# One layer of a hybrid attention encoder on one core: softmax and delta-rule attention interleaved, short convolution and head norms moved into the input products

## The chip, the core and the metric

The kernel runs on one core of a Trainium2 chip. The metric is the device time of one execution in microseconds (us). The engines are called PE (TensorE matmul; PEld is its weight load), DVE (VectorE), ACT (ScalarE), POOL (GpSimd) and SP (the queue that issues most loads). Each engine runs its own instructions in order and waits for others by semaphores. Operands live in SBUF; PE writes PSUM, which has eight banks here, LP 0 to 3 and MP 0 to 3.

## The reference, cut to what matters

Two layers are computed for 512 prompt frames and 32 sample frames (N = 544 tokens), width 1024, all float32. Only the first layer's mixer is touched. Cut to its core:

```python
qkv_a, z_a, b_a, a_a, q_b, k_b, v_b, f_b = split(rmsnorm(x) @ w_in)
qkv_a = silu(causal_conv(qkv_a, width 4))           # 12 rows of 128 channels
qa, ka = l2norm(qa), l2norm(ka)                     # 4 heads each: 8 rows
oa = gated_delta_rule(qa, ka, va, g, beta, s0)      # chunks of 64 tokens, WY form
oa = rmsnorm(oa) * silu(z_a)
ob = fox_attention(q_b, k_b, v_b, log_forget)       # softmax, 4 heads, blocks of 128 queries
x = x + concat(oa, ob) @ w_out
```

Per chunk and head the delta rule inverts a 64x64 triangular matrix (here by doubling: blocks of 2, 4, ... 32), forms u and w with it, and then carries a 128x128 state from chunk to chunk. Everything behind this mixer (cross-attention, MLP, the second layer) is the same before and after.

## The kernel before

**Weights.** A product with a 1024-row weight is made in panels of 256 columns (two tiles of 128 columns). SP loads a panel into `stage`, ACT copies its high part to `wh` (`split`, L1291), POOL subtracts to get the low part `wl` (`low_parts`, L616), and PE makes each tile with three products per 128 rows (`block`, L717). There are two slots of each, so the split of a panel is made right after the product of the panel two before it. A tile may begin once the tile two before it has been drained from LP by DVE (L768).

**Stages of the first mixer, in order.** (1) `in_a`: 16 tiles; DVE drains 12 rows into `ua` (`four_conv_rows`, L1936) and 4 into `z`; 48 small gate products stand after the fourth tile (L895). (2) `in_b`: 12 tiles into kb_f, vb_f, qb_f; behind each drain DVE makes the 4-tap convolution of one `ua` row into `sq` (L1998 to L2016, eight instructions), and ACT applies Silu (L1470), which needs an activation table of its own (loads at L1450 and L1479). Between the panels PE transposes k and v (`turned`, L909). (3) `forget_rows(False)` (L936) sums the log-forget rows on PE, and the cached keys are transposed (L971). (4) `attention("fox_p")`: 16 units of softmax attention, and beside them, through the hooks `delta_sums`, `delta_rstds` and `delta_scales` (L978, L1501, L2018), the l2norm of the 8 q and k rows. (5) `forget_rows(True)`, (6) `attention("fox_s")`: 4 units for the sample tokens. (7) The delta rule: chunk sums (L1002), then the list `DELTA` (L446), which every engine walks in the same order: 63 steps `inv` of the inverses (`inverse`: gram, turns, x and d per size, uw), 19 steps `turn` (`turn_in`: transposes and forget rows, through one bank), 36 steps `rec` (`recurrence`: ws, qs, ds, o per chunk). The last 16 steps are the recurrence of tiles 2 and 3 alone. (8) `out0`: the first half of the products can run at once; the other half waits for the norm and gate of the delta output (L1624 on ACT, L1113 on DVE).

**Softmax pipeline.** `attention` (L794 on PE, L1337 on ACT, L1815 on DVE) runs over i: PE transposes the probabilities of unit i-2, multiplies values of i-3, makes scores of i+1; DVE scales the scores (L1843), masks, takes the maximum, later normalises; ACT takes the exponential (L1347) and copies (L1370, L1379). Scores, transposes and values each alternate between two banks.

Of the kernel before, what the change touches and what calls it, by code (L numbers as in the profile page):

```python
# [5 lines left out]
def build_program(nc, t):  # L6
# [71 lines left out]
    with ctx:  # L78
# [20 lines left out]
        xl = place("xl", [128, KT, N], f32r)  # L99
        stage = [place(f"stage{s}", [128, 2048]) for s in range(2)]  # L100
# [85 lines left out]
        def region(at):  # L186
# [19 lines left out]
        delta_buf, delta_end = region(delta_at)  # L206

        LT, Tm, TmT, Xm = [[delta_buf(f"{n}{c}", [128, H, 64 if c < 2 else NS]) for c in range(3)]
                           for n in ("LT", "Tm", "TmT", "Xm")]
        BT = [delta_buf(f"BT{c}", [128, 2, H, 64 if c < 2 else NS]) for c in range(3)]  # L210
        dec = Xm
        AT = [delta_buf(f"AT{j}", [128, H, 64 if j < TT else NS]) for j in range(NTOK)]

        kd = [place(f"kd{j}", [128, H, 128], at=xh_at + 4 * H * 128 * j) for j in range(TT)] + [
            delta_buf("kd_s", [128, H, 128])]
        vbt = [place(f"vbt{j}", [128, H, 128], at=xl_at + 4 * H * 128 * j) for j in range(TT)] + [
            delta_buf("vbt_s", [128, H, 128])]
        um = [place(f"um{j}", [128, H, 128], at=xl_at + 4 * H * 128 * j) for j in range(TT)] + [
            delta_buf("um_s", [128, H, 128])]
        assert 4 * H * 128 * TT <= 4 * H * N  # L220
        at = delta_end[0]
        kbe = [delta_buf(f"kbe{j}", [128, H, 128]) for j in range(NTOK)]
        wT = [place(f"wT{j}", [128, H, 128 if j < TT else NS], at=at + 4 * H * 128 * j) for j in range(NTOK)]
        grow = delta_buf("grow", [128, 2, H, 128])
        vnew = delta_buf("vnew", [128, H, 128])

        S = delta_buf("S", [128, 4, H, 128])
        gsm = delta_buf("gsm", [128, NTOK, 16])
        neg_g = delta_buf("neg_g", [128, NTOK, H])
        eg = delta_buf("eg", [128, NTOK, 2, H])  # L230
        o_a = ua[:, 2 * H:3 * H, 0:N]
        assert delta_end[0] <= gates_start, (delta_end[0], gates_start)
# [74 lines left out]
        neg_ready = sem("neg_ready")  # L307
# [99 lines left out]

        def out_bank(U, u):
            bank = MP[0:U["D"], 2 + u % 2, 0:U["P"] * U["G"]]
            return bank.rearrange("p (g n) -> p g n", g=U["G"]) if U["G"] > 1 else bank  # L410
# [14 lines left out]
        def steps_of(j):  # L425
            sizes = sizes_of(j)
            pe = ["gram", "turns"]
            dve = ["lower", "gram"]
            for n in sizes:
                pe += [f"x{n}"] + ([f"dt{n}"] if n != sizes[-1] else []) + [f"dtt{n}"]  # L430
                dve += ([f"dt{n}"] if n != sizes[-1] else []) + [f"dtt{n}"]
            return pe + ["uw"], ["gram", "turns"] + [f"x{n}" for n in sizes] + ["uw"], dve
# [3 lines left out]
        def count_of(steps, name, r):  # L436
# [4 lines left out]
        TURNS = [(kind, j) for kind in ("k", "v", "g") for j in (0, 1, TT)] + [  # L441
            ("w", 0), ("w", 1)] + [(kind, j) for kind in ("g", "k", "v", "w") for j in (2, 3)]
# [3 lines left out]
        def delta_order():  # L446
# [3 lines left out]
            turns = [("turn",) + t for t in TURNS if t[0] != "w"]  # L450
            recs = [("rec", name, j, c) for j, c in CHUNKS for name in ("ws", "qs", "ds", "o")]
            for r, tiles in enumerate(((0, 1, TT), (2, 3))):
                names = ["gram", "turns"] + [f"{w}{n}" for n in SIZES for w in ("x", "d")] + ["uw"]
                later = [x for x in recs if r and x[2] in (0, 1, TT)]
                for i, name in enumerate(names):
                    for j in tiles:
# [4 lines left out]
                        if name == "uw" and j < TT:  # L461
                            out.append(("turn", "w", j))
# [11 lines left out]
        def inv_bank(j, k):  # L474

            return LP[:, 2 * STREAM[j] + k, :] if j < TT else MP[:, 2 + k, :]
# [31 lines left out]
        def _(sp):  # L508
# [70 lines left out]
            first_pair("out0")  # L579
# [5 lines left out]

            sp.wait_ge(arena_free, 1)
# [20 lines left out]
        def _(pool):  # L607
# [79 lines left out]
            with pool.Fori(2, LIN["out0"][0] // 2 + 1) as i:  # L687
# [20 lines left out]
            with pool.Fori(LIN["out0"][0] // 2 + 1, PANELS // 2) as i:  # L708
# [5 lines left out]
        def _(pe):  # L714
# [79 lines left out]
            def attention(name, also=lambda i: None):  # L794
                u0, count = GROUP[name]

                def scores(u):
                    U = UNITS[u]
                    if u >= 2:
# [1476 lines left out]
```

## Time and profile before

| | us |
|---|---|
| median of 3 runs (1750.8 to 1761.66) | 1759.62 |
| the profiled execution, its own time | 1760.79 |
| its span in the trace | 1759.0 |
| PE busy, PEld busy | 1667.0, 1568.5 |
| DVE, ACT, POOL busy | 765.3, 607.2, 531.3 |

The span runs from the first to the last instruction of the trace; the execution's own time is 1.8 us more. A busy share of PE counts a matmul from its start to its modelled end. Times inside the trace are given from the span's start. The stretches of the first mixer in it: in_a 36.3 to 127.7, in_b to 211.9, forget rows and cached keys to 232.8, fox_p to 275.9, forget rows to 291.8, fox_s to 310.4, delta rule to 436.4 (its first round of inverses to 362.6, the second with recurrence steps between to 418.8, the last recurrence steps alone to 436.4), then out0.

### The profile page before, as it was taken

To read this page: it belongs to the slowest core of one execution; us is meant where nothing else is said; L and a number is where in the kernel's file an instruction comes from. 1 tells how busy PE (TensorE), PEld (TensorE's weight loads), DVE (VectorE), ACT (ScalarE), POOL (GpSimd) and SP (SyncE) were. 2 spreads that over 40 slices of the span, in tenths; PEclk is the share of its full clock that TensorE was granted. 3 is DMA by queue.
4 is the path that set the end of the run, shared out by engine and by line. 5 is a ranking of instruction groups with operands and counts; after the bars stand their busy time and mean duration, and the time that the engine had idled before them with its cause. 6 is when DMAs were issued, how large, how long until landed. Compare 5 with 4: busy or idle time off the path is not lost.

```text
span 1759.0 us, 31567 instructions
## 1 busy us (share of the span) xinstructions
PE 1667.0 (95%) x13326; PEld 1568.5 (89%) x13326; DVE 765.3 (44%) x1403; ACT 607.2 (35%) x1120; POOL 531.3 (30%) x187
## 2 busy tenths in 40 slices
PE   6999888999988999999999999989889999999998
PEld 6999756888887899999999997559878999999998
DVE  4119753443574632222223623784746322223235
ACT  4113373221443442222223314783434323222232
POOL 4533300210252133443433432002621443433441
PEclk9999998899999999999999998899999999999999
DMA  5232300000433023223222223001320223222221
GB/s 150 74 95 76 119 26 1 8 2 13 144 114 103 25 72 97 82 87 96 89 78 95 73 96 133 1 1 49 120 97 25 80 89 97 90 78 95 81 86 51
DMA packets 123034, 131.39 MB, mean 75 GB/s; under 512 B 6285, under 2 KB 115122, under 8 KB 122930
## 3 DMA queue, kind: packets, MB, share of 16 engines
q1 hardware_dynamic: 116064, 123.27, 21.5%
q10 hardware_dynamic: 6866, 6.63, 1.2%
q8 instruction: 77, 1.26, 0.3%
q14 instruction: 27, 0.22, 0.0%
HBM read 122.44 MB, written 7.45 MB: 74 GB/s over the span
## 4 chain that ended last, share of the span: by engine, by line
PE 84%; DVE 10%; ACT 3%; issue 2%; DMA 0%; ACTq 0%; DVEq 0%
PE LP L722 66%; PE MP L839 3%; PE LP L1044 3%; PE LP L805 3%; PE MP L823 2%; DVE acc L1790 1%; DVE sq L2014 1%; PE LP L957 1%; DVE sq L2012 1%; DVE xl L1797 1%; PE MP L1138 1%; DVE probs L1856 1%; PE MP L1124 1%; PE MP L1132 0%; DMA stage<-in_w_in_ab 0%
## 5 line engine op out<-in xcount | busy, mean ns | idle before, releaser
L619 POOL TENSOR_TENSOR wl<-stage,wh 128x2048 fp32r<-128x2048 f32 x107 | 493.5, 4612 | 1017.5 <-ACT wh L1294 1017.4
L722 PE MATMUL LP<-xh,wh 128*128 128x272 f32 x2176 | 458.3, 292 | 14.3 <-DVE xl L1797 7.2
L722 PE MATMUL LP<-xh,wl 128*128 128x272 f32 x2176 | 452.9, 290 | 0.0
L722 PE MATMUL LP<-xl,wh 128*128 128x272 f32 x2176 | 452.3, 290 | 0.0
L1294 ACT CAST wh<-stage 128x2048 fp32r<-128x2048 f32 x107 | 203.7, 1904 | 462.7 <-PE LP L722 461.9
L722 PEld LDWEIGHTS LP<-xh,wh 128*128 128x128 f32 x2176 | 345.6, 190 | 19.3 <-DVE xl L1797 9.7
L722 PEld LDWEIGHTS LP<-xl,wh 128*128 128x128 f32 x2176 | 345.7, 191 | 0.0
L722 PEld LDWEIGHTS LP<-xh,wl 128*128 128x128 f32 x2176 | 342.9, 190 | 0.0
L722 PE MATMUL LP<-hh,wh 128*128 128x272 f32 x1024 | 211.2, 287 | 0.0
L722 PE MATMUL LP<-hh,wl 128*128 128x272 f32 x1024 | 210.6, 288 | 0.0
L722 PE MATMUL LP<-hl,wh 128*128 128x272 f32 x1024 | 210.3, 287 | 0.0
L2176 DVE TENSOR_TENSOR hsq<-rel 128x544 f32<-128x544 f32 x64 | 70.1, 1095 | 267.9 <-ACT rel L1701 261.4
L722 PEld LDWEIGHTS LP<-hl,wh 128*128 128x128 f32 x1024 | 160.1, 188 | 0.0
L722 PEld LDWEIGHTS LP<-hh,wh 128*128 128x128 f32 x1024 | 159.4, 188 | 0.0
L722 PEld LDWEIGHTS LP<-hh,wl 128*128 128x128 f32 x1024 | 159.4, 188 | 0.0
L2191 DVE TENSOR_TENSOR dtmp<-LP,rstd 128x544 f32<-128x544 f32 x64 | 46.3, 724 | 234.8 <-PE LP L722 234.8
L1701 ACT ACTIVATE rel<-LP 128x544 f32<-128x544 f32 x64 | 39.9, 624 | 237.3 <-PE LP L722 237.3
L1790 DVE TENSOR_TENSOR acc<-acc,sq 128x544 f32<-128x544 f32 x49 | 81.8, 1670 | 23.4 <-ACT sq L1319 23.4
L1797 DVE SCALAR_TENSOR_TENSOR xl<-x,cols,xh 128x544 fp32r<-128x544 f32 x48 | 78.4, 1644 | 23.9 <-ACT xh L1324 23.7
L1319 ACT ACTIVATE sq<-x 128x544 f32<-128x544 f32 x56 | 36.8, 658 | 138.2 <-DVE x L1811 75.0
L699 POOL TENSOR_TENSOR BT<-LT,level 128x256 f32<-128x256 f32 (+1 forms) x24 | 18.1, 768 | 160.8 <-DVE LT L2076 132.3
L823 PEld LDWEIGHTS MP<-ident,probs 128*128 128x128 f32 (+2 forms) x284 | 32.2, 151 | 30.8 <-DVE probs L1887 19.5
(357 smaller groups left out, 1877.7 us busy)
## 6 DMA issues: line engine op xcount, KB each, us to landing
stage<-in_w_up SPq DMA_DIRECT2D x32, 1024.0 KB, 5.3
stage<-in_w_down SPq DMA_DIRECT2D x32, 1024.0 KB, 5.2
stage<-in_w_in_ab SPq DMA_DIRECT2D x13, 1024.0 KB, 5.2
stage<-in_w_xkv SPq DMA_DIRECT2D x8, 1024.0 KB, 5.4
stage<-in_w_in_c SPq DMA_DIRECT2D x6, 1024.0 KB, 5.0
stage<-in_w_out_ab SPq DMA_DIRECT2D x4, 1024.0 KB, 7.1
stage<-in_w_xq SPq DMA_DIRECT2D x4, 1024.0 KB, 5.6
stage<-in_w_xo SPq DMA_DIRECT2D x4, 1024.0 KB, 5.9
```

What stands on the lines that cost most here:

```text
L619: pool.tensor_tensor(wl[s][:, :], stage[s][:, :], wh[s][:, :].bitcast(f32), ALU.subtract).then_inc(w_lo, 1)
L722: mm = pe.matmul(LP[:, 2 * slot + half, 0:b - a], weights, X[part][:, k, a:b], start=(first and n_ == 0), stop=(last and n_ == 2), skip_gr ...
L805: mm = pe.matmul(LP[0:U["P"], 2 * (u % 2) + at // 512, at % 512:at % 512 + n], U["q"][g], kT, start=True, stop=True, skip_group_check=True)
L823: mm = pe.transpose(MP[0:n, u % 2, to:to + P], probs_of(u, slice(at, at + n)), ident[0:P, 0:P])
L839: mm = pe.matmul(MP[0:U["D"], 2 + u % 2, g * P:g * P + w], v[g], U["PT"][0:n, u % 2, at:at + w], start=(c == 0), stop=(c == last), skip_gr ...
L1044: return pe.matmul(out, lhsT, rhs, start=start, stop=stop, skip_group_check=True)
L1294: act.copy(wh[s][:, :], stage[s][:, :]).then_inc(w_hi, 1)
L1701: act.activation(rel[:, k % 2, :].rearrange("p (a n) -> p a n", a=2), LP[:, 2 * (k % 2):2 * (k % 2) + 2, 0:HALF], ACT.Relu).then_inc(relu_ ...
L1790: dve.tensor_tensor(acc[:, :], acc[:, :], sq[:, k % 2, :], ALU.add).then_inc(sq_used, 1)
L1797: dve.scalar_tensor_tensor(out=xl[:, k, :], in0=x[:, k, :], scalar=gain(n_, k), in1=xh[:, k, :].bitcast(f32), op0=ALU.mult, op1=ALU.subtra ...
L2176: dve.tensor_tensor(hsq[:, k % 2, :], rel[:, k % 2, :], rel[:, k % 2, :], ALU.mult).then_inc(hsq_ready, 1)
L2191: dve.tensor_tensor(two(dtmp[:, k % 2, :]), banks(k), two(rstd[:, :]), ALU.mult).then_inc(drained, 1)
```

## The change

**Layout and banks.** The buffers of the delta rule move into `stage`, `wh` and `wl`, so that softmax and delta rule can be live together; kbe, wT, vbt and um lie in `ua` itself. So the first two panels of `out0` are loaded only after the last turn. The inverse has one bank per tile (MP 0, 1), turns have MP 3, the recurrence MP 2 and LP 3; softmax has LP 0 for scores, LP 1 for transposes, LP 2 for values, one each. The two updates of a doubling step become one DVE instruction; q and w become turns of their own (25 turns).

**Input products.** The convolution and Silu of each row go behind its drain in `in_a`; the l2norm goes into `in_b`, its PE sums in the panel breaks.

**Attention.** One walk: `attention` gets a hook `beside`, which runs 6 steps of DELTA in each of 18 rounds of fox_p, and the last 16 steps in 6 rounds of fox_s.

```diff
+        LATE = [x for x in DELTA if x[0] == "rec" and x[2] in (2, 3)]
+        BESIDE = {"fox_p": spread(DELTA[:len(DELTA) - len(LATE)], 0, 18), "fox_s": spread(LATE, 0, 6)}
+        def beside(name, inverse, turn_in, recurrence):
+            def go(i):
+                for what in BESIDE[name].get(i, ()):
+                    {"inv": inverse, "turn": turn_in, "rec": recurrence}[what[0]](*what[1:])
+            return go
...
-            first_pair("out0")
...
+            sp.wait_ge(turn_used, len(TURNS))
+            first_pair("out0")
...
                 def scores(u):
-                    if u >= 2:
+                    if fox:
+                        pe.wait_ge(sc_used, u)
+                    elif u >= 2:
...
                     pe.wait_ge(p_ready, u + 1)
-                    if u >= 2:
+                    if fox:
+                        pe.wait_ge(pt_ready, u)
+                    elif u >= 2:
...
-            one_pair("in_b", 0, XS)
-            pe.wait_ge(conv_dve, 1)
+            pe.wait_ge(conv_dve, CW * NCONV)
...
+            def head_sums(first, last):
+                def go():
+                    for f in range(first, last):
+                        pe.wait_ge(head_sq, f + 1)
+                        if f >= 2:
+                            pe.wait_ge(head_ln, f - 1)
+                        for half, (a, b) in enumerate(TOKENS):
+                            mm = pe.matmul(MP[:, 2 * (f % 2) + half, 0:HALF], ones[:, :], sq[:, f % 2, a:b], ...)
+                        mm.then_inc(head_sum, 1)
+                return go
+            one_pair("in_b", 0, XS, between=head_sums(0, 2))
+            head_sums(2, 5)()
+            one_pair("in_b", 1, XS, between=head_sums(5, 2 * H))
+            pe.wait_ge(head_ln, 2 * H)
...
-            attention("fox_p", delta_sums)
-            pe.wait_ge(head_ln, 2 * H)
-            forget_rows(True)
-            attention("fox_s")
...
+            attention("fox_p", beside("fox_p", inverse, turn_in, recurrence))
+            forget_rows(True)
+            pe.wait_ge(rows_act, 2 * H)
+            attention("fox_s", beside("fox_s", inverse, turn_in, recurrence))
...
-            product("in_a")
+            act.preload_act_table_set("silu_and_others")
+            for T in range(NCONV + H):
+                if T % 2:
+                    split_after("in_a", T)
+                if 1 <= T <= NCONV:
+                    act.wait_ge(conv_dve, CW * T)
+                    act.activation(ua[:, T - 1, 0:N], sq[:, (T - 1) % 2, :], ACT.Silu).then_inc(conv_act, 1)
+            act.wait_ge(drained, DRAINED["in_b"])
+            act.activation(z[:, :, :], z[:, :, :], ACT.Silu).then_inc(conv_act, 1)
+            act.preload_act_table_set("natural_log_exp_and_others")
...
+            split(0, 16 * (LIN["out0"][0] // 2 + 1))
+            attention("fox_s", beside("fox_s", inverse, turn_in, recurrence))
...
                     head_rstd(2 * H + h - 1, 1.0 / HD)
+                if h == 1:
+                    split(1, 16 * (LIN["out0"][0] // 2 + 1))
...
+                dve.tensor_copy(conv_new[:, 0, :, f], ua[:, f, NPT:NPT + PAD])
+                dve.tensor_copy(conv_new[:, 1, :, f], ua[:, f, UPAD - PAD:UPAD])
+                for i in range(CW):
...
                 dve.tensor_tensor(two((kb_f, vb_f, qb_f)[f // H][:, f % H, :]), banks(f), two(rstd[:, :]), ALU.mult)
-                for i in range(CW):
...
+                for m in {2: (0, 1), 4: (2, 3, 4), 6: (5, 6, 7)}.get(f, ()):
+                    dve.wait_ge(head_exp, m + 1)
+                    dve.scalar_tensor_tensor(out=ua[:, m, 0:N], in0=ua[:, m, 0:N], in1=head_squares[:, m % 2, :], ...)
```

`spread(items, first, steps)` cuts a list into `steps` nearly equal parts. On ACT a row's norm in `in_b` is `row_rstd` (Ln and Exp into `head_squares`) and `head_square`; rows 0 and 1 are squared before `in_b`'s loop, the norms of rows 0 and 1 stand after tile 1, of 2 to 4 after tile 3, of 5 to 7 after tile 5. On DVE, fox_p begins after the chunk sums have come back from ACT.

## Rows read from the trace of the kernel before

**Rows 1.** The page: busy shares, and the chain that ended last
```profile
PE 1667.0 (95%) x13326; PEld 1568.5 (89%) x13326; DVE 765.3 (44%) x1403; ACT 607.2 (35%) x1120; POOL 531.3 (30%) x187
...
PE 84%; DVE 10%; ACT 3%; issue 2%; DMA 0%; ACTq 0%; DVEq 0%
```
**Rows 2.** Stretch, its length, busy PE PEld DVE ACT POOL, clock; stages in order
```profile
36.30:127.70 91.40, 91.29 (x728) 89.38 (x728) 13.12 (x41) 13.37 (x7) 45.54 (x53) 1.00 0.30 93
127.70:211.90 84.20, 80.21 (x622) 79.26 (x622) 73.53 (x120) 27.62 (x37) 28.23 (x6) 0.96 0.24 77
211.90:232.80 20.90, 13.54 (x48) 8.63 (x49) 8.30 (x9) 8.05 (x11) 4.50 (x1) 0.84 0.27 101
232.80:275.90 43.10, 34.66 (x184) 25.59 (x184) 32.60 (x104) 33.37 (x96) 0.00 (x0) 0.96 0.07 27
275.90:291.80 15.90, 15.72 (x72) 11.32 (x72) 0.00 (x0) 2.06 (x6) 0.00 (x0) 0.89 0.00 1
291.80:310.40 18.60, 15.50 (x76) 11.80 (x76) 8.84 (x28) 5.68 (x22) 0.00 (x0) 0.72 0.00 1
310.40:362.60 52.20, 49.03 (x860) 42.95 (x860) 22.36 (x54) 13.59 (x45) 9.37 (x14) 0.86 0.03 8
362.60:418.80 56.20, 55.91 (x849) 49.51 (x848) 25.21 (x59) 12.25 (x33) 8.72 (x10) 0.95 0.01 2
418.80:436.40 17.60, 15.76 (x130) 14.88 (x128) 7.23 (x20) 1.99 (x5) 0.00 (x0) 1.00 0.00 1
436.40:453.10 16.70, 13.73 (x63) 11.59 (x64) 8.64 (x12) 9.82 (x16) 0.00 (x0) 0.80 0.84 283
397.00:412.00 15.00, 15.00 (x256) 13.70 (x256) 6.74 (x18) 2.07 (x5) 0.23 (x1) 1.00 0.01 2
```
**Rows 3.** Timeline of DVE in in_a: drain of a row (first and last), two drains of z
```profile
36.30 0.43 DVE L1941 TENSOR_TENSOR ua<-LP,rstd 128x272 f32<-128x272 f32 x1
37.22 0.44 DVE L1941 TENSOR_TENSOR ua<-LP,rstd 128x272 f32<-128x272 f32 x1
...
109.70 0.72 DVE L1954 TENSOR_TENSOR z<-LP,rstd 128x544 f32<-128x544 f32 x1 [5.03 <-PE LP L722]
115.71 0.72 DVE L1954 TENSOR_TENSOR z<-LP,rstd 128x544 f32<-128x544 f32 x1 [5.29 <-PE LP L722]
```
**Rows 4.** Timeline of DVE in in_b: a convolution's first instruction, the next drain, a long instruction
```profile
137.69 0.48 DVE L2008 TENSOR_SCALAR sq<-ua,cols 128x512 f32<-128x512 f32 x1
...
141.09 0.72 DVE L2000 TENSOR_TENSOR kb_f<-LP,rstd 128x544 f32<-128x544 f32 x1
...
144.01 4.59 DVE L2014 SCALAR_TENSOR_TENSOR sq<-ua,cols,sq 128x32 f32<-128x32 f32 x1
```
**Rows 5.** Timeline of POOL: low parts of a panel in in_a and in in_b
```profile
105.67 4.61 POOL L619 TENSOR_TENSOR wl<-stage,wh 128x2048 fp32r<-128x2048 f32 x1 [7.34 <-ACT wh L1294]
...
143.74 4.81 POOL L619 TENSOR_TENSOR wl<-stage,wh 128x2048 fp32r<-128x2048 f32 x1 [9.41 <-ACT wh L1294]
```
**Rows 6.** Timeline of PE: k turns, forget rows, the sums of one head row
```profile
181.43 1.03 PE L915 MATMUL MP<-ident,kb_f 128*32 128x128 f32 x4 [3.21 <-ACT k_out L1459]
...
222.96 7.21 PE L957 MATMUL LP<-upper,gates_raw 128*128 128x512 f32 x16 [5.71 <-ACT nF L1484]
...
250.72 1.16 PE L987 MATMUL LP<-head_squares,ones 128*128 128x272 f32 x4 [0.45 <-ACT rstd L1512]
```
**Rows 7.** Timeline of DVE in out0: the first head's norm and gain
```profile
443.66 0.78 DVE L2117 SCALAR_TENSOR_TENSOR ua<-ua,cols,rstd 128x544 f32<-128x544 f32 x1 [7.56 <-ACT rstd L1540]
```
**Rows 8.** Groups in fox_p: busy, mean ns, idle before and its releaser
```profile
L1843 DVE SCALAR_TENSOR_TENSOR probs<-LP,nF 128x128 f32<-128x128 f32 (+3 forms) x16 | 7.8, 485 | 13.8 <-PE LP L805 13.8
L1851 DVE TENSOR_REDUCE nm<-probs 128x1 f32<-128x128 f32 (+3 forms) x16 | 7.7, 480 | 0.0
L1848 DVE TENSOR_TENSOR probs<-probs,diag_mask 128x128 f32<-128x128 f32 x16 | 4.6, 285 | 0.0
...
L1347 ACT ACTIVATE probs<-probs,nm 128x128 f32<-128x128 f32 (+3 forms) x16 | 9.0, 562 | 6.4 <-DVE nm L1851 6.3
...
L1379 ACT CAST xh<-MP 128x128 fp32r<-128x128 f32 x16 | 4.0, 250 | 0.4 <-PE MP L839 0.4
...
L1347 ACT ACTIVATION_READ_ACCUMULATOR probs<-probs,nm 128x1 f32 x16 | 3.0, 188 | 0.0
```
**Rows 9.** Groups over 0 to 560: the delta rule's copy of x
```profile
L1601 ACT COPY Xm<-LP 128x256 f32<-128x256 f32 x20 | 7.2, 373 | 27.9 <-PE LP L1044 27.6
```

More of the change, by code:

```diff
@@ new lines, in build_program, with in_rows @@
+        um_s = place("um_s", [128, H, 128], at=stage_at + 5 * slot + 4 * H * 128)
+        wT_s = place("wT_s", [128, H, NS], at=stage_at + 5 * slot + 8 * H * 128)
+        vnew = sample_buf("vnew", [128, H, 128])
+        assert sample_end[0] <= stage_at + 6 * slot
+        def in_rows(first):
+            return [ua[:, first:first + H, 128 * j:128 * j + 128] for j in range(TT)]
+        kbe, wT, vbt, um = (in_rows(H) + [kbe_s], in_rows(H) + [wT_s], in_rows(2 * H) + [vbt_s], in_rows(2 * H) + [um_s])
@@ L449, in delta_order @@
             out = []
-            turns = [("turn",) + t for t in TURNS if t[0] != "w"]
+            turns = [("turn",) + t for t in TURNS if t[0] not in "qw"]
             recs = [("rec", name, j, c) for j, c in CHUNKS for name in ("ws", "qs", "ds", "o")]
@@ L472, in build_program, with inv_bank, spread @@
         assert sum(x[0] == "turn" for x in DELTA) == len(TURNS)
-        def inv_bank(j, k):
-            return LP[:, 2 * STREAM[j] + k, :] if j < TT else MP[:, 2 + k, :]
+        def inv_bank(j):
+            return MP[:, STREAM[j], :]
+        TURN_BANK, W_BANK, O_BANK = MP[:, 3, :], MP[:, 2, :], LP[:, 3, :]
+        def spread(items, first, steps):
+            return {first + i: items[len(items) * i // steps:len(items) * (i + 1) // steps] for i in range(steps)}
+        LATE = [x for x in DELTA if x[0] == "rec" and x[2] in (2, 3)]
[5 more added lines that the diff above has]
+            return go
         def chunks_of(j):
@@ L685, in _ @@
             assert n[0] == MASKS, n[0]
-            with pool.Fori(2, LIN["out0"][0] // 2 + 1) as i:
+            with pool.Fori(2, LIN["out0"][0] // 2) as i:
                 for s in range(2):
@@ L706, in _ @@
                     level_mask(what[2], SIZES.index(int(what[1][1:])) + 1)
[L708 removed]
+            with pool.Fori(LIN["out0"][0] // 2, PANELS // 2) as i:
                 for s in range(2):
@@ L1369, in pt @@
                     full = sum(n_ == 128 for n_, _ in U["v"])
-                    inst = act.copy(U["PT"][:, s, 0:full * w], MP[:, s, 0:full * w])
+                    bank = LP[:, 1, :] if U["kind"] == "fox" else MP[:, s, :]
+                    inst = act.copy(U["PT"][:, s, 0:full * w], bank[:, 0:full * w])
                     if full < len(U["v"]):
                         rows = U["v"][-1][0]
-                        inst = act.copy(U["PT"][0:rows, s, full * w:full * w + w], MP[0:rows, s, full * w:full * w + w])
+                        inst = act.copy(U["PT"][0:rows, s, full * w:full * w + w], bank[0:rows, full * w:full * w + w])
                     inst.then_inc(pt_ready, 1)
@@ L1611, in recurrence @@
                     act.wait_ge(rec_pe, 4 * CHUNKS.index((j, c)) + 4)
[L1612 removed]
+                    act.copy(o_a[:, :, a:a + P], O_BANK[:, 0:H * P].rearrange("p (h n) -> p h n", h=H)
                              ).then_inc(rec_act, 1)
[L1615 to L1616 removed]
+            attention("fox_p", beside("fox_p", inverse, turn_in, recurrence))
+            act.wait_ge(ol_ready, sum(GROUP["fox_p"]))
+            forget_rows(True)
+            split(0, 16 * (LIN["out0"][0] // 2 + 1))
+            attention("fox_s", beside("fox_s", inverse, turn_in, recurrence))
+            act.wait_ge(ol_ready, sum(GROUP["fox_s"]))
             act.wait_ge(rec_dve, 2 * len(CHUNKS))
             store(t["o_p_gdn_state"][0, 0].rearrange("h k v -> k h v"), S[:, 0, :, :])
[L1619 removed]
+            store(t["o_s_gdn_state"][0, 0].rearrange("h k v -> k h v"), S[:, 1, :, :])
             act.wait_ge(rec_act, NTOK)
```

456 lines of the change are left out of this document (212 added, 244 removed).

## The prediction

> **What bounds the kernel now.** The page first: PE is busy for 95% of the span, and 84% of the chain that ended last is PE [rows 1]. So time can come only from stretches where PE waits, runs at the lower clock, or does work that goes. The busy time by stretch gives them [rows 2]. In in_a PE is full (91.29 of 91.40 us), a tile comes each 6.01 us (z drains at 109.70 and 115.71) and DVE is idle for 78 us [rows 3]. In in_b DVE is busy for 73.53 of 84.20 us, since the convolution is there. Between in_b and fox_p PE works 13.54 of 20.90 us. From fox_p to the end of the delta rule (232.8 to 436.4, 203.6 us) PE is busy for 186.5 us and its weight loads for 156.0: little idle time, at a mean clock below 1. The change touches nothing behind out0, so the sum is that of six stretches.
>
> **1. in_a: the convolution comes in, +6 us.** Per row DVE now drains (36.30 to 37.22, 0.92 us [rows 3]), copies two edges (my estimate 0.25, from two small instructions; 0 to 0.5) and convolves (137.69 to 141.09, 3.40 us [rows 4]): 4.57 us, 9.1 per panel of two tiles, below the 12.0 that PE needs. But an instruction of POOL takes DVE's time. The low part of a panel runs 4.6 us, and a 128x32 convolution step that met one took 4.59 us where its neighbours take a quarter of one; a z drain from PSUM at 109.70 inside POOL's 105.67 to 110.28 took its usual 0.72 [rows 3 to 5]. So DVE loses up to 4.4 us a panel and needs 13.5. PE runs 12.0. The lag is bounded: tile 13 may start at 109.7 once row 11 is drained. DVE starts at 36.3; eleven rows (50.3), one drain (0.9), the gate row (0.7), six low parts in the way (4.2 each, 25) and some 3.5 for POOL's small mask instructions give 116.7, so PE loses 7.0; with 0.92 of a drain hidden under each low part it is 1.5. I take 6, nearer the full block; range +1 to +9. Silu on ACT (12 times 0.66) has room there: ACT is busy for 13 of 91 us.
>
> **2. in_b: the convolution goes, the head norms come, +6 us.** DVE falls to a drain a tile. PE gains 8 rows of sums. One takes 1.16 us with its tail, some 1.0 in a stream [rows 6]: +8.0. They stand between panels, and PE waits in two places for a square that ACT makes only after the split (1.9), Ln, Exp and Square (0.65 each) with 2 or 3 sums in between: 1.9 each, +3.8 (0 to 6). What goes: PE's 3.21 us wait for ACT at the k turns [rows 6], since ACT no longer sits behind a Silu, and the lower clock that followed it (tile 8 was made in 182.4 to 190.7, 8.3 for 6.0): -5.5. Together +6.3, range +1 to +10. The gate chain at in_b's start stays: POOL's low part holds it today as well, and ACT's Silu of z fits beside.
>
> **3. Forget rows, first time, -4 us.** PE waited 5.71 us there for ACT, which was behind the last convolution [rows 6], and ACT loaded a table. Now: eight long matmuls a head, 2.3 us, 9.2 for four; 0.8 before; key turns through two banks with ACT copies 3.0; the chunk sums 2.7, their way through ACT and DVE 1.4: DVE's first softmax step at 17.1 after the last drain instead of 21.4. -4.3, and the sums' 2.9 leave the delta rule. Range -2 to -7.
>
> **4. fox_p beside the delta rule, -11.5 us.** Before: 43.1 + 52.2 + 56.2 = 151.5 us [rows 2]. PE's work in it, from the timeline at the full clock: softmax per head 2.2 scores, 1.4 transposes, 2.5 values, 24.4 for four heads (the head sums are gone); first round of inverses 42 (52.2 less the chunk sums, 4.5 of waiting and 8 from the lower clock); second 53. With some 4 us for the switches: 124, 6.9 a round over 18 rounds. What is added are waits. Softmax has one bank each, so scores of i+1 wait for DVE's scaling of i, which stands behind DVE's delta work of the round before: about 0.6 to 0.8 us a round after PE's transposes and values (1.0) are done. An ACT copy of a delta step stands behind the exponential, which waits for scaling, mask and maximum (0.49 + 0.29 + 0.48 [rows 8]); PE's three or four items before it mostly cover that. In the first round DVE has three tiles' chains of five instructions before its next scaling: 3 us. 18 x 0.75 + 3 = 16.5: 140 us. Queued behind such a wait on PE is all of the round's delta work, so nothing fills it. DVE has 27 + 48 of 140 us, ACT less; neither binds. Range 128 to 160 us, so -23 to +8.
>
> The page Perfetto Trace Analysis of the Trainium skill (Identifying the Most-Contended Engine) says to judge TensorE by the busy share of its weight loads, because pipelined matmuls hide gaps. By that, 203.6 - 156.0 = 48 us would be idle in the whole block, not 17. The trace agrees only in part: in 397 to 412, where PE never waits, the loads are busy for 13.70 of 15.00 us [rows 2], so 156.0 stand for 171. That row carries the first rival below.
>
> **5. Forget rows and fox_s with the last recurrence, 0 us.** Before 15.9 + 18.6 + 17.6 = 52.1. PE's work in the last two is 28 at the full clock, but the chain is short of cover: four units over six rounds. The first out0 panel is now split here and its low part runs in DVE's way. That no row shows for these operations; the nearest are the blocked step and the free drain [rows 4, 3]: +0 to +4.4. I take the block, since mask and normalisation have both inputs in SBUF or are of the kind that met it: 36 for 36. Range -8 to +5. The page SBUF — State Buffer of the Trainium skill (Who interferes with whom) says that a VectorE instruction with two SBUF inputs waits for the whole of a GpSimd instruction that reads SBUF, a reduction does not; by that the mask is held and the maximum waits behind it in the queue too, the same 4.4.
>
> **6. Start of out0, +4.4 us.** The second split (1.9) now stands between the norms of the heads, and its low part (4.6) follows right after DVE's first gain at 443.66 [rows 7]. The second comes at 450 instead of 445.5. Covered today: both panels were split long before. Range +1 to +6.
>
> **Sum:** 6 + 6.3 - 4.3 - 11.5 + 0 + 4.4 = +0.9. The profiled execution took 1760.8 (1759.0 and 1.8 around it), 1.2 above the median 1759.6; 1761.7 by its clock, 1760 as a median. So no change that a measurement of this kernel can tell (about 1%, 17.6 us).
>
> **Rivals.** *A: PE runs solid.* Delta steps cover softmax's waits and the clock stays up: 124 in part 4, 28 in part 5: 16 and 8 less; half of parts 1 and 2 with it, 6: 1730. For it: 171 of 203.6 us, and DVE's small load. Against: one bank each, and a strict order on four engines.
> *B: the round boundary decides.* PE gets its first delta step only when the whole chain has run: a DVE delta step (0.7), scaling, mask, maximum (0.49, 0.29, 0.48), exponential (0.56 and 0.19 for its sum), softmax's copy (0.25) and the delta copy (0.37) [rows 8, 9]: 3.3 us, less the 1.0 of softmax work on PE beside it, is 2.3, 1.6 more than the 0.75 in my sum. Over 24 rounds +38: 1798. It decides from 0.75 us more a round (+17.6). For it: in fox_s such a chain leaves PE at a clock of 0.72 [rows 2]. Against: six items stand between, and most need no copy of their own round.
> *C: DVE binds the input products.* Every low part blocks fully and PE falls behind by 1.5 a panel in in_a, with part 6 at its upper end: +10 more than my sum in all, 1771, still within 1%.
> *D: the interleaving gives nothing*, PE being 95% busy already: part 4 is 151.5 less the chain sums' 2.9, 148.6, and part 5 as now: 1769.
>
> **Chances.** Forecast 0.32, C 0.1, D 0.1 (these three within 1%, less their tails), A 0.26, B 0.22. Range 1733 to 1787; the forecast's own 1748 to 1773. Faster 0.27, same 0.49, slower 0.24.
>
> **What would show it.** In the changed profile in_a ends 3 to 9 us later with DVE as PE's releaser once or twice; convolution steps of 4.6 us stand in in_a; in_b has two waits of PE for `sq`; the fused fox_p lasts 135 to 147 us with the clock above 0.95 and waits of PE for `probs` or `nm` below 1 us each; DVE's second gain in out0 comes 6 us after the first. Wrong if the fused part is below 128 (A) or above 160 (B), or if PE's idle time in in_a is nil.

## The result, and the profile after

The changed kernel takes 1813.42 us (median of 4, 1810.11 to 1816.63), the kernel before 1760.64 (median of 4): a ratio of 1.031 with an interval of 1.025 to 1.036, 53 us slower. The forecast was 1760, the range 1733 to 1787; it lies outside. The profiled execution took 1816.63 us, its span is 1814.8 against 1759.0.

The page first, to hold beside [rows 1]: the engines' busy times and the chain that ended last.

```profile
PE 1695.8 (93%) x13326; PEld 1591.6 (88%) x13326; DVE 763.7 (42%) x1406; ACT 611.1 (34%) x1112; POOL 533.7 (29%) x187
...
PE 85%; DVE 10%; issue 2%; ACT 2%; DMA 0%; ACTq 0%; DVEq 0%
```

The number of matmuls is the same (13326), and PE is busy for 28.8 us more, at a mean granted clock of 0.949 for 0.966. So the page already tells that idle time alone cannot explain the 56 us, and points to the clock. The stretches of the changed kernel, as in [rows 2] (length, busy time of PE, PEld, DVE, ACT and POOL, granted clock, DMA share, GB/s): in_a, in_b, forget rows and cached keys, fox_p with 108 delta items, forget rows, fox_s with the last recurrence, start of out0.

```profile
36.00:132.60 96.60, 92.35 (x733) 90.01 (x732) 77.16 (x161) 21.54 (x20) 49.02 (x54) 1.00 0.29 88
132.60:224.10 91.50, 86.70 (x655) 84.17 (x654) 17.87 (x38) 33.86 (x48) 22.89 (x5) 0.98 0.15 48
224.10:238.30 14.20, 12.48 (x63) 8.70 (x63) 1.26 (x3) 4.43 (x8) 0.00 (x0) 1.00 0.54 186
238.30:421.20 182.90, 150.61 (x1846) 125.00 (x1845) 71.21 (x187) 47.91 (x144) 18.17 (x24) 0.81 0.02 6
421.20:436.00 14.80, 14.03 (x73) 10.45 (x73) 0.00 (x0) 2.79 (x9) 0.00 (x0) 1.00 0.43 142
436.00:485.90 49.90, 43.44 (x205) 36.72 (x205) 20.10 (x48) 8.34 (x23) 4.51 (x1) 0.61 0.00 1
485.90:509.60 23.70, 16.86 (x78) 14.83 (x79) 11.10 (x12) 11.73 (x17) 4.52 (x1) 0.74 0.59 200
```

Against [rows 2], by the six steps of the prediction (the first mixer ends at the first drain of out0, at 455.0 before and 509.6 after; behind it 1300.1 and 1301.1 us, unchanged; in_a is counted from 36.0 in both):

| step | forecast | measured |
|---|---|---|
| 1 in_a | +6 | +4.9 |
| 2 in_b | +6.3 | +7.3 |
| 3 forget rows, first time | -4.3 | -6.7 |
| 4 fox_p beside the delta rule (151.5 before) | -11.5 | +31.4 |
| 5 forget rows, fox_s, last recurrence (52.1 before) | 0 | +12.6 |
| 6 start of out0 | +4.4 | +5.1 |
| behind it | 0 | +1.0 |

The loss is in steps 4 and 5. To see what kind of time it is, each stretch is cut in three parts: time in which PE is idle; half of the busy time that lies in the lower clock level (what the clock cost, since that level is half of the full clock); the rest, PE's work at the full clock. The clock intervals are the trace's record of the granted clock, which knows two levels, 2.4 and 1.2 GHz.

| stretch | us | work | idle | clock |
|---|---|---|---|---|
| before, fox_p to the last recurrence | 203.7 | 168.4 | 17.0 | 18.2 |
| changed, the same (238.3 to 485.9) | 247.6 | 159.1 | 39.5 | 48.9 |
| of it fox_p with 108 items | 182.9 | 119.6 | 32.3 | 31.0 |
| of it fox_s with 16 items | 49.9 | 25.5 | 6.5 | 17.9 |

The work is near what I had (119.6 for 124, 25.5 for 28). In later runs with the same PE instructions in the same order it reads 120.2 to 122.1 in fox_p, so the cut is good to some 2 us. Idle time grew by 22.5 us and the clock's cost by 30.7. Who waited in the fused fox_p: the list of PE's waits (line waiting, what it waited for, us in total, times, longest).

```profile
PE LP L885 <- DVE xl L1934: 23.0, 11, 3.4
PE LP L847 <- DVE probs L1883: 6.7, 4, 3.9
PE MP L1085 <- ACT ua L1605: 0.9, 1, 0.9
```

The wait that I had priced, scores for `probs`, is the second line. The first one stands in no step of mine: values (L885) of one unit wait for the low part `xl` of the unit before, because there is one output bank. One round of the timeline shows why it comes late. DVE, from the last delta steps of the round:

```profile
374.39 0.69 DVE L2122 TENSOR_TENSOR T<-T,MP 128x512 f32<-128x512 f32 x1 [0.40 <-PE MP L1101]
377.56 1.12 DVE L2135 SCALAR_TENSOR_TENSOR S<-S,eg,MP 128x128 f32<-128x128 f32 x4 [2.48 <-PE MP L1181]
378.60 0.55 DVE L1883 SCALAR_TENSOR_TENSOR probs<-LP,nF 128x384 f32<-128x384 f32 x1
379.06 0.15 DVE L1923 RECIPROCAL rr<-rs 128x1 f32<-128x1 f32 x1
379.18 0.29 DVE L1889 TENSOR_TENSOR probs<-probs,diag_mask 128x128 f32<-128x128 f32 x1
379.39 0.35 DVE L1928 TENSOR_SCALAR probs<-probs,rr 128x256 f32<-128x256 f32 x1
379.65 0.55 DVE L1892 TENSOR_REDUCE nm<-probs 128x1 f32<-128x384 f32 x1
380.11 0.28 DVE L1934 TENSOR_TENSOR xl<-LP,xh 128x128 fp32r<-128x128 f32 x1
```

PE in the same microseconds: the round's last delta item, one turn, and the values.

```profile
376.36 1.16 PE L1181 MATMUL MP<-vnew,kd 64*128 64x128 f32 x8
377.45 0.33 PE L867 MATMUL LP<-ident,probs 128*128 128x128 f32 x1
380.54 2.05 PE L885 MATMUL LP<-PT,vb_n 128*128 128x128 f32 x8 [2.76 <-DVE xl L1934]
```

DVE sits idle until PE's last delta item ends, then makes that item's step, then the whole softmax block, and the low part last: 377.56 to 380.39 with nothing on PE but a turn of 0.33. The low part itself needs 0.28 us, and its input was ready at 372.0 (ACT's high part, a cast of 0.27 us at 371.76). At the end of the wait PE's values run at half clock (2.05 us where the same eight took 1.16 at 419.30 in this trace).

In fox_s the first mask is held by POOL's low part of out0's first panel; first DVE's row, then POOL's, then PE's scores that wait for it:

```profile
437.95 4.40 DVE L1889 TENSOR_TENSOR probs<-probs,diag_mask 32x32 f32<-32x32 f32 x1
...
437.81 4.51 POOL L649 TENSOR_TENSOR wl<-stage,wh 128x2048 fp32r<-128x2048 f32 x1 [51.58 <-ACT wh L1340]
...
444.44 1.91 PE L847 MATMUL LP<-kpT,qb_f 128*32 128x512 f32 x2 [3.44 <-DVE probs L1883]
```

Other masks of 32x32 take 0.18. From 443.8 on the clock is low, in two intervals of 23.9 and 20.5 us: 38.6 of the stretch's 49.9 us.

The input products behave as forecast, and the start of out0 nearly. PE's longest waits in in_a and in in_b:

```profile
PE LP L752 <- DVE ua L1982: 4.1, 2, 2.5
...
PE MP L979 <- ACT sq L1515: 4.0, 2, 2.0
```

In DVE's timeline a convolution step and an edge copy that POOL's low parts hold in in_a (neighbours take 0.25 and 0.17), and out0's second gain, held for 2.5 us by the low part that POOL began at 495.94 (it begins 3.6 us after the first, at 494.11, and not 6; its end is held to 501.0):

```profile
96.89 4.56 DVE L2003 SCALAR_TENSOR_TENSOR sq<-ua,cols,sq 128x32 f32<-128x32 f32 x1
...
111.11 4.11 DVE L1989 COPY conv_new<-ua 128x3 f32<-128x3 f32 x1
...
497.74 3.30 DVE L2147 SCALAR_TENSOR_TENSOR ua<-ua,cols,acc 128x544 f32<-128x544 f32 x1 [2.09 <-ACT acc L1581]
```

### The profile page after: what moved, and what is told of

It is laid out like the page before. It is cut to its first block, busy times and chain, and to the rows that moved or that the text cites. A ratio compares the mean times of both kernels' runs of the same rounds, so it can differ in the third digit from the quotient of the medians.

```text
span 1814.8 us, 31483 instructions
## 1 busy us (share of the span) xinstructions
PE 1695.8 (93%) x13326; PEld 1591.6 (88%) x13326; DVE 763.7 (42%) x1406; ACT 611.1 (34%) x1112; POOL 533.7 (29%) x187
## 4 chain that ended last, share of the span: by engine, by line
PE 85%; DVE 10%; issue 2%; ACT 2%; DMA 0%; ACTq 0%; DVEq 0%
PE LP L752 64%; PE LP L847 4%; PE MP L1101 3%; PE MP L885 3%; PE MP L867 2%; DVE acc L1829 1%; PE LP L885 1%; PE LP L1020 1%; DVE xl L1836 1%; DVE sq L2003 1%; PE MP L1181 1%; PE MP L1167 1%; DVE sq L2001 1%; PE LP L1185 1%; DVE probs L1897 1%
## 5 line engine op out<-in xcount | busy, mean ns | idle before, releaser
L1340 ACT CAST wh<-stage 128x2048 fp32r<-128x2048 f32 x107 | 203.7, 1904 | 422.6 <-PE LP L752 422.6
L1365 ACT ACTIVATE sq<-x 128x544 f32<-128x544 f32 x56 | 36.8, 657 | 138.1 <-DVE x L1850 74.9
L729 POOL TENSOR_TENSOR BT<-LT,level 128x256 f32<-128x256 f32 (+1 forms) x24 | 18.2, 769 | 166.7 <-DVE LT L2090 98.5
L1393 ACT ACTIVATE probs<-probs,nm 128x256 f32<-128x256 f32 (+4 forms) x100 | 48.4, 484 | 35.7 <-DVE nm L1892 32.9
```

Source lines behind the costliest of these rows:

```text
L1340: act.copy(wh[s][:, :], stage[s][:, :]).then_inc(w_hi, 1)
L1393: inst = act.activation(probs_of(u, at), LP[0:P, 2 * s, at] if cross else probs_of(u, at), ACT.Exp, bias=nm[0:P, u % 3, g:g + 1], scale=U[ ...
```

## The experiments

The theory (W) after this reading: the round boundary is one chain that ends in the low part, and the low clock is its consequence. Its rivals: the clock falls because of the mix of short matmuls (C1); the wait only moves (C2); delta items would wait instead (C3); the single banks cost the time, not the interleaving (C4). The median of the kernel before beside the first three runs was 1755.04.

**The low part first.**

```diff
+                    if i > lag + 1 and name[:3] == "fox":
+                        low(u0 + i - lag - 2)
                     turns = ([scored(u0 + i)] if i < count else []) + (
...
-                    if i > lag + 1:
+                    if i > lag + 1 and name[:3] != "fox":
                         low(u0 + i - lag - 2)
                     also(i)
```

> Edit: on VectorE the low part of a finished head output (L1934) goes ahead of the round's softmax steps instead of behind them; nothing else. Theory W (each round of the fused stage is closed by one chain: last delta step on VectorE, scaling, mask, maximum, reciprocal, normalisation, low part, and only then may TensorE's values overwrite the one output bank): the eleven waits of TensorE's L885 for xl, 23.0 us in all, fall to under 8 us; the low clock is a consequence of these waits, so its cost in the fused fox_p (31.0 us) falls by about half as well; fused fox_p from 182.9 to about 150 us, time about 1782. Rival C1 (the low clock comes from the mix of short matmuls, not from the waits): the waits fall, the low clock stays, time about 1798. Rival C2 (the wait only moves to the next scores, which need the scaling behind the same VectorE queue): waits for probs (6.7 us) grow to 20 or more, time 1808 to 1815.

1787.12 us, ratio 1.019 (1.017 to 1.021): 26 us below the changed kernel's 1813.42. By the ratios (1.031 and 1.019) it is 20 us, since the kernel before was 5.6 us faster beside this run. The fused fox_p:

```profile
239.90:393.00 153.10, 134.43 (x1847) 111.67 (x1846) 70.86 (x187) 46.10 (x144) 18.12 (x24) 0.91 0.03 8
```

PE's two largest waits from 230 to 500:

```profile
PE LP L847 <- DVE probs L1883: 12.0, 7, 3.9
PE LP L885 <- DVE xl L1934: 7.2, 7, 2.2
```

The waits for xl fell from 23.0 to 7.2; those for probs did not grow (the 12.0 are fox_p and fox_s together, and were 12.0 before: 6.7 and 5.3). Idle 32.3 to 18.7, clock cost 31.0 to 12.4. For fox_p W holds, C2 falls, and C1 with it: the PE instructions and their order are the same, and the clock came back where waits went. The clock's share of the gain (18.6) is larger than that of the waits (13.6). fox_s with the last recurrence gained nothing: it took 52.4 us for 49.9, with the same wait of 3.4 us and a longer low clock.

**The softmax block in the middle.** On DVE (first part of the diff) and ACT (second) it stands behind the third of the six delta items of the round before.

```diff
+                    for i in range(-1, count + lag + 1):
+                        also(i, slice(0, 3))
+                        turns = ([scored(u0 + i + 1)] if i + 1 < count else []) + (
+                            [normed(u0 + i)] if 0 <= i < count else [])
...
+                        if i > lag:
+                            low(u0 + i - lag - 1)
+                        also(i, slice(3, None))
...
+                for i in range(-1, count + lag + 1) if name[:3] == "fox" else ():
...
+                    also(i, slice(0, 3))
+                    if i + 1 < count:
+                        exps(u0 + i + 1)
+                    also(i, slice(3, None))
```

> Edit: on VectorE and ScalarE the softmax block of a round stands in the middle of the previous round's six delta items (behind the third) instead of behind the sixth; same instructions, same order on TensorE. Theory W: the block has half a round of delta work on TensorE as cover, so no wait of TensorE for xl or probs stays above 1 us; idle time in the fused fox_p from 32.3 to about 8 us, its clock above 0.93; fused fox_p about 134 us, fused fox_s with the last recurrence from 49.9 to about 41; time about 1757. Rival C1 (low clock from the mix): idle as above, but the low clock keeps its 31.0 and 17.9 us: about 1783. Rival C3 (two microseconds of softmax ahead of the delta steps on VectorE and ScalarE make TensorE's delta items wait instead): waits for the delta tiles of 1 to 2 us in every round, time 1795 to 1815.

1767.28 us for the 1757 expected, ratio 1.0075 (1.0058 to 1.0092). The fused fox_p, and fox_s with the last recurrence:

```profile
239.70:370.40 130.70, 125.79 (x1845) 106.96 (x1845) 70.65 (x187) 44.82 (x144) 18.33 (x24) 0.96 0.03 9
...
386.90:439.30 52.40, 46.14 (x205) 39.41 (x205) 20.09 (x48) 8.12 (x23) 4.50 (x1) 0.57 0.00 1
```

130.7 for the 134 expected; cut in three it is 121.0 work, 4.9 idle, 4.8 clock. That is 20.8 us less than the 151.5 of the kernel before, more than step 4 had promised. But 7.1 of them are PE work that the change put into other stages (the same cut gives the kernel before 128.1 of work there; the head sums now stand in in_b). Idle time and clock give 13.7. So the interleaving works once softmax has delta work as cover. In DVE's timeline the low part now has delta steps close on both sides of its block:

```profile
324.62 0.68 DVE L2150 TENSOR_TENSOR vnew<-ua,MP 64x512 f32<-64x512 f32 x1 [0.28 <-PE MP L1167]
...
326.34 0.28 DVE L1943 TENSOR_TENSOR xl<-LP,xh 128x128 fp32r<-128x128 f32 x1
326.53 0.68 DVE L2142 TENSOR_TENSOR T<-T,MP 128x512 f32<-128x512 f32 x1
```

My expectation of 41 us for fox_s failed: 52.4, since the mask's block stays and the clock is low for 44.9 us behind it (see the first split early).

**Apart.**

```diff
-        BESIDE = {"fox_p": spread(DELTA[:len(DELTA) - len(LATE)], 0, 18), "fox_s": spread(LATE, 0, 6)}
+        BESIDE = {"fox_p": {18: DELTA[:len(DELTA) - len(LATE)]}, "fox_s": {6: LATE}}
```

> Edit: the delta items are not spread over the softmax rounds: 108 of them stand behind fox_p's last round and 16 behind fox_s's last; all other parts of the change stay, the single banks too. This prices the interleaving itself. Theory W: fox_p alone at one bank each about 57 us (18 rounds of some 3.2 us), the delta rule's 108 items 105, forget rows 15, fox_s about 24, last recurrence 17.6: 219 us where the changed kernel takes 247.6; time about 1786. Rival C4 (the interleaving gains what it covers, and the single banks cost the time): fox_p alone 80 us or more, time 1810 or more. Of the change there then stay the input products, the forget rows and out0's start, together +3.3 us by the two profiles.

1811.46 us, no different from the changed kernel: the time that C4 gave, not W's 1786. But the four executions spread widely (1803.4, 1804.5, 1818.4, 1820.3), and the profile is of the slowest. fox_p alone, the 108 items alone, fox_s with the last recurrence behind it:

```profile
238.30:305.70 67.40, 44.98 (x153) 30.15 (x152) 27.80 (x97) 21.08 (x67) 0.00 (x0) 0.62 0.04 13
305.70:406.00 100.30, 95.85 (x1694) 85.26 (x1693) 44.43 (x90) 26.99 (x77) 18.06 (x24) 1.00 0.01 2
...
422.50:477.20 54.70, 47.00 (x205) 40.74 (x205) 20.40 (x48) 8.30 (x23) 4.50 (x1) 0.54 0.00 0
```

PE's largest wait in fox_p alone (238 to 300):

```profile
PE LP L885 <- DVE xl L1934: 18.1, 12, 2.2
```

By the stretches each theory has part of it. fox_p alone at one bank each takes 67.4 us (25.6 work, 22.4 idle, 19.4 clock), where two banks gave 43.1 [rows 2]: 24 us more, although its work is 7.4 us less. Two things differ from the kernel before, the banks and the head sums, which no longer fill waits; the values' wait for `xl`, which was 1.0 us in all before, suggests that the banks are most of it. The 67.4 are less than the 80 that C4 wanted and more than my 57. The delta rule alone never left the full clock (100.3 us, 1.00). 67.4 + 100.3 = 167.7 is 15 us less than the 182.9 of the interleaved order: as built, interleaving was worse than none in this stretch. Against the same 167.7 the block in the middle (130.7) gains 37.0 us; that is what the interleaving is worth with single banks. The whole span is no shorter here for two reasons in this profile: fox_s with the recurrence took 4.8 more, and the unchanged part behind out0's start 13 more (the last section).

**The place of the block.** This run is as the run with the block in the middle, but ahead of all six items.

```diff
-                        also(i, slice(0, 3))
+                        also(i, slice(0, 0))
...
-                        also(i, slice(3, None))
+                        also(i, slice(0, None))
```

> Edit on the changed kernel: as the run with the softmax block in the middle of the round's six delta items, but the block stands ahead of all six (on VectorE and ScalarE), so that only its place in the round differs. Theory W: softmax has the whole round as cover, but the round's first delta steps wait behind 2 us of it, so TensorE's delta items wait in many rounds: fused fox_p about 138 us against 130.7, time 1770 to 1778. Rival: TensorE's first delta items of a round need nothing of the same round, and the place makes no difference: 1765 to 1768.

1769.21 us, ratio 1.0045 (1.0014 to 1.0076), the median before 1760.97 beside this run and the next three. The fused fox_p, and a wait in it:

```profile
238.50:373.10 134.60, 126.25 (x1846) 106.64 (x1846) 71.93 (x187) 45.59 (x144) 17.92 (x24) 0.95 0.02 8
...
PE MP L1085 <- DVE kd L2124: 2.3, 1, 2.3
```

134.6 us lies between the two expectations. Idle is 8.4 for 4.9, with one wait of a delta turn (L1085) for DVE's `kd` of 2.3 us that the middle doesn't have. By these profiles the place within the round matters by 4 us, too little for the medians to tell; that the block isn't last matters by 48 to 52.

**The first split early**, on top of the middle.

```diff
                     inst.then_inc(rows_act, 1)
+                    if sample and h == 1:
+                        split(0, 16 * (LIN["out0"][0] // 2 + 1))
...
             forget_rows(True)
-            split(0, 16 * (LIN["out0"][0] // 2 + 1))
```

> Edit, on top of the run with the softmax block in the middle: ScalarE makes the split of out0's first panel inside the second forget rows (behind the second head's copies) and not right ahead of fox_s, so that POOL's low part (4.5 us) ends before fox_s's first mask, which it held for 4.40 us of VectorE there. In that run fox_s with the last recurrence took 52.4 us: 25.1 of work, 6.3 idle, 21.0 lost to a low clock that began 1 us before the end of that wait and stood for 47.8 us, although TensorE was busy from then on. Theory W (the low clock follows the wait): the wait of 3.4 us goes and the clock stays up, 52.4 falls to 30 to 34 us; time about 1746. Rival C1 (fox_s's thin matmuls beside recurrences of 64 columns lower the clock by themselves): only the 3 us of the wait go, clock cost stays near 18 to 21 us; time about 1764. Rival: the split on ScalarE delays the third and fourth head's rows, forget rows 2 us longer, nothing gained.

1759.21 us, ratio 0.9993 (0.9965 to 1.0021). The first mask of fox_s in DVE's timeline:

```profile
386.70 0.18 DVE L1899 TENSOR_TENSOR probs<-probs,diag_mask 32x32 f32<-32x32 f32 x1
```

fox_s with the last recurrence:

```profile
384.80:426.80 42.00, 37.94 (x205) 32.98 (x205) 15.96 (x48) 6.28 (x22) 0.00 (x0) 0.70 0.00 1
```

The block is gone (0.18 for 4.40), and 52.4 became 42.0: 2.2 of idle time and 9.1 of clock (work reads 0.9 more). Neither theory had it (30 to 34, or only the 3 us of the wait): the clock still fell at 401.9 and stayed down for 30.7 us. So here W has part of it, and C1 may have the rest; which is not shown. The rounds of fox_s are thin, and after waits of 1.2 us and less for probs the clock fell and did not come back, although PE then had one wait of 0.5 us to the end.

**The second split late**, on top of it.

```diff
-                if h == 1:
-                    split(1, 16 * (LIN["out0"][0] // 2 + 1))
                 if h >= 2:
                     act.wait_ge(head_y, h - 1)
                     act.copy(xh[:, h - 2, :], o_a[:, h - 2, :]).then_inc(head_hi, 1)
+            split(1, 16 * (LIN["out0"][0] // 2 + 1))
```

> Edit, on top of the previous run: the split of out0's second panel stands behind the last head's high part and not between the norms, so that neither its 1.9 us of ScalarE nor POOL's low part stands in the way of the gains. My step 6 says the start of out0 lost 4.4 us to them (5.1 measured from the two profiles): out0's start falls from 22.6 to about 19 us, 3.5 less than the run before it. Rival: the low part now comes too late for the second panel, and TensorE waits for wl: 0 to 3 us more.

1756.07 us, ratio 0.9986 (0.9959 to 1.0013). The start of out0:

```profile
426.70:445.00 18.30, 15.31 (x78) 13.24 (x79) 8.67 (x12) 11.63 (x17) 0.65 (x1) 0.83 0.59 201
```

18.3 us where the run before it had 23.8 and the kernel before 18.6: the whole of step 6 was this placement, and no wait for wl came in its place.

**The convolution lags one row**, on top of it.

```diff
+                if f:
+                    convolve(f - 1)
...
-                if 1 <= T <= NCONV:
-                    act.wait_ge(conv_dve, CW * T)
...
+                if 2 <= T <= NCONV + 1:
+                    act.wait_ge(conv_dve, CW * (T - 1))
...
```

> Edit, on top of the previous run: in in_a VectorE drains row f+1 before it convolves row f (ScalarE's Silu follows one tile later). My step 1 says that in_a is 4.9 us longer because POOL's low parts hold VectorE and TensorE then waits for a drain twice, 4.1 us in all. A drain reads PSUM and is not held, so with one row of lag both waits go: in_a from 96.6 to 92.4 us, 4 less than the run before it. Rival: the lag only defers the wait, since VectorE needs 13.5 us for every 12 of TensorE: one wait of about 2 us stays.

in_a of this run:

```profile
36.00:129.80 93.80, 92.19 (x734) 90.07 (x733) 76.94 (x162) 21.52 (x21) 49.48 (x54) 1.00 0.30 90
```

PE's one wait in it:

```profile
PE LP L752 <- DVE ua L2021: 1.5, 1, 1.5
```

From 4.1 us in two waits to 1.5 in one, as the rival said; in_a is 2.8 shorter than in the changed kernel, not 4. The median is 1759.64, ratio 0.9987 (0.9949 to 1.0025): too noisy to show it.

**The last recurrence sooner**, on top of it: 16 items over four rounds of fox_s.

```diff
-        BESIDE = {"fox_p": spread(DELTA[:len(DELTA) - len(LATE)], 0, 18), "fox_s": spread(LATE, 0, 6)}
+        BESIDE = {"fox_p": spread(DELTA[:len(DELTA) - len(LATE)], 0, 18), "fox_s": spread(LATE, 0, 4)}
```

> Edit, on top of the run with the lagging convolution: the 16 last recurrence items stand in the first four rounds of fox_s, four a round (one chunk), and not over six rounds. There fox_s with the last recurrence took 43.4 us: 26.0 of work, 4.1 idle (2.7 of it in three waits for probs in the first rounds), 13.3 lost to a low clock of 27 us. Theory W: four items a round cover those waits, idle falls by 2 us and the clock cost by half or more: 33 to 38 us, 6 to 10 less than the run before. Rival: four items of one chunk are one chain (each waits for VectorE), they cover nothing, and the last softmax rounds then stand bare: 43 to 48 us, same or slower.

**The last recurrence behind fox_s**, in its place.

```diff
-        BESIDE = {"fox_p": spread(DELTA[:len(DELTA) - len(LATE)], 0, 18), "fox_s": spread(LATE, 0, 6)}
+        BESIDE = {"fox_p": spread(DELTA[:len(DELTA) - len(LATE)], 0, 18), "fox_s": {6: LATE}}
```

> Edit, on top of the run with the lagging convolution: the 16 last recurrence items stand behind fox_s's last round. It prices that half of the interleaving alone. With everything apart and the early split missing, fox_s with the last recurrence took 54.7 us (54.6 of it at the low clock); before the change 18.6 + 17.6 = 36.2 us. Theory W: beside the recurrence 43.4 us; apart one bank each leaves fox_s's chain bare, about 25 us at the low clock for most of it, and then 17 of recurrence at the full clock or 30 at half: 42 to 52 us, so the interleaving gains 0 to 9 us here. Rival: apart is faster, since the recurrence runs at the full clock as before the change: 36 to 40 us.

fox_s with the last recurrence, over four rounds:

```profile
379.10:420.50 41.40, 37.52 (x204) 30.92 (x204) 15.95 (x48) 6.06 (x22) 0.00 (x0) 0.69 0.00 1
```

And behind fox_s:

```profile
380.50:424.20 43.70, 37.20 (x205) 32.52 (x205) 16.18 (x48) 6.28 (x22) 0.00 (x0) 0.73 0.00 0
```

41.4 and 43.7 us, where six rounds gave 43.4. Four a round gain 2.0, not 6 to 10 (a miss), and apart is no worse: in fox_s the interleaving over six rounds is worth nothing. (The expectation's "54.6 of it at the low clock" is the whole low interval of the run apart; 50.4 of it lie in the 54.7 us.) Medians 1751.64 (ratio 0.9984, 0.9957 to 1.0010) and 1759.47 (1.0015, 0.9993 to 1.0038), the kernel before beside them 1756.84. So the best order of the change that I found equals the kernel before within what can be measured. In its profile (1749.82 us) out0's first drain comes at 439.5, 15.4 us earlier than before, but the unchanged part behind it takes 4.4 us more. The interval of the ratio leaves room for a gain of 7.6 us at most, so the 15.4 do not reach the time in full. Why, is not shown; the last section has the spread of that part.

## Why the prediction was wrong

- **What bounds the kernel, and steps 1, 2, 3, 6: right in the main.** Releasers, places and numbers came near what was foretold: DVE's drain twice in in_a, two waits for `sq` in in_b (4.0 us for my 3.8), the held gain. Step 3 was low by 2.4 us. Together +10.6 for +12.4.
- **Step 4, the work: near.** 119.6 us for 124. The 42 us for the first round of inverses do not follow from the terms beside them: 52.2 less 2.9 (chunk sums), 4.5 and 8 is 36.8, and with that the work would have been 118.
- **Step 4, the waits: the step that failed first.** It said that "scores of i+1 wait for DVE's scaling of i", 0.75 us a round, 16.5 in all. That wait is there (6.7 us). What ended last was another: values of i-3 need the low part of i-4 to be out of the one output bank, and DVE makes it at the end of its block, behind the round's last delta step. It cost 1.4 to 3.4 us in eleven of the 18 rounds, 23.0 in all; idle time was 32.3, twice my sum. I followed the bank of the scores and had not asked the same of the other two. The run with the low part first takes 15.8 us of this wait away by moving one instruction of 0.28 us.
- **Step 4, the clock: the term that was missing.** The sum took PE's work at the full clock and added waits. 31.0 of the 182.9 us are the clock. Four kernels with the same PE instructions in the same order have idle 32.3, 18.7, 8.4 and 4.9 us in this stretch and a clock cost of 31.0, 12.4, 6.1 and 4.8: a microsecond of waiting in the softmax rounds cost another 0.7 to 1.0. The 108 delta items alone had 4.5 us of idle time and no such cost. The profile of before held it: fox_s, a chain with short waits, ran at 0.72, and the first round of inverses at 0.86 [rows 2]; I even cited the first for rival B and subtracted 8 us from the second as if interleaving would lift it.
- **Step 5.** The block by the low part came as said (4.40 us for 4.4), the work nearly (25.5 for 28). "36 for 36" came out as 49.9, of which 17.9 are the clock, which fell during a wait of 3.44 us. With the block in the middle this stretch took 52.4, and the split made early gave 10.4 of them back.
- **Rivals.** B had the right place, "the round boundary decides". Its chain went through the exponential to the delta copy, which the six items do cover (no wait of PE for that copy in the fused fox_p is over 0.2 us); the true one goes through DVE alone. It had no clock term either, so that its 1798 lies nearer to 1813 than the forecast is in part luck: its 38 us were all waiting, and idle time grew by 22.5. A falls as built, but its 124 for the fused part is not far from the 130.7 with the block in the middle. C was not what decided: in_a and the start of out0 took 10.0 us more, for 10.4 forecast. D, the interleaving gives nothing, had 148.6 for the fused part: as built it lost 31.4 us against the kernel before, and in another order it gained.
- **The page on the busy share of weight loads** (the Trainium skill, Perfetto Trace Analysis, Identifying the Most-Contended Engine) leaves 48 us of headroom where I saw 17 idle. The experiments side with my reading: with most waits gone the block still took 186.7 us at its best for 203.6 (233.8 to 420.5 in the run with the recurrence sooner: 161.1 work, 10.9 idle, 14.7 clock). The same page's Optimization Strategy says that interleaving two regimes may improve performance. The trace agrees only in some orders: with the block in the middle fox_p is 20.8 us shorter than before (13.7 without the moved work), and as the change was written it was 31.4 longer.
- **SBUF — State Buffer of the Trainium skill** (Who interferes with whom) says that a VectorE operation with two SBUF inputs, or a copy in a two-port mode, is blocked for the whole of a GpSimd instruction that reads SBUF and was issued first. The trace agrees: behind a POOL instruction that had just begun, the mask took 4.40 us for 0.18 and a copy of three columns 4.11 for 0.17 (its mode the trace doesn't show); a z drain from PSUM at 126.63, inside POOL's 122.60 to 127.20, kept its 0.72.

Open: whether two halves of the one output bank would do as well as the order. I wrote that kernel and expected 1778 to 1785 us, but have no measurement of it: DVE would read the bank while PE writes it, with nothing to order the two. Open too: why the clock in fox_s stays low with PE hardly idle.

## What to carry to other kernels

When two pipelines are interleaved with single buffers, list for each buffer the instruction that frees it and what stands ahead of that instruction in its engine's queue; put the freeing instruction, and the whole of the other pipeline's block, into the middle of the filler work, not behind its last item (here ahead of the first item cost 4 us, behind the last 52). Where short waits come back in rounds of short matmuls, look at the granted clock too: in the fused rounds here such a wait cost 1.7 to 2.0 times its length. Whether that holds in another kernel has to be measured. And place long POOL instructions that read SBUF where DVE is idle: two moves of one line gave 10.4 and 5.5 us of their stretches, most of the first by the clock.

## What the runs showed that I had not expected

The clock fell nine times in the fused fox_p between 260 and 421 us although no single wait there was longer than 3.4 us and those for xl were mostly 1.4 to 2.8. And once low it can outlast its cause. In code that the change doesn't touch, the sliding-window attention of the second layer, the same instructions met the lower level for 17.1 us in most profiles and for 51.2 us in three (the runs apart, with the second split late, and with the lagging convolution). The 34.1 us behind the first 17.1, in the run with the first split early:

```profile
1094.90:1129.00 34.10, 31.10 (x172) 19.17 (x170) 29.17 (x126) 28.88 (x111) 0.00 (x0) 1.00 0.01 1
```

And in the run with the second split late:

```profile
1088.40:1122.50 34.10, 34.10 (x107) 19.13 (x105) 18.89 (x81) 19.07 (x72) 0.00 (x0) 0.50 0.00 1
```

At half clock PE gets through 107 matmuls and is never idle; at full clock through 172, idle for 3 us. So a PE that is busy for the whole of a stretch can still be slow, and the stretch behind out0's start took 1301.2 us in one run and 1312.9 in the other: 12 us of difference in code that no edit touches, and more than several of the gains measured here. There is one profile of each kernel, so it is not shown what makes this stretch go one way or the other, nor how often it does.
